# Convolution, output gate and new keys and values made beside the projection's products; level products from 64 rows per head

## The reference

```python
x = LN(x);  z = x @ w_in              # 3088 columns: gq gk gv gr glow sq sk sv cb cc ch
# A: gated linear attention, 4 heads, dk 64, dv 128, chunks of 64 tokens
lg  = log_sigmoid(glow @ w_gate_up + b_gate) / 16;  b = cumsum(lg) in a chunk
att = sum_k q[t,k] k[s,k] exp(b[t,k] - b[s,k]),  s <= t
o   = (q exp(b)) S + att v;   S = exp(b_last) S + (k exp(b_last - b))^T v
go  = rms_norm(o) * gla_norm_g * silu(gr)
# B: stick-breaking attention, 4 heads x 64, causal, over all keys up to t
so  = sum_s sigmoid(z[t,s]) prod_{s<r<t} (1 - sigmoid(z[t,r])) v[s],  z = q k / 8
# C: u = cc * ch;  co = cb * (w2 u[t] + w1 u[t-1] + w0 u[t-2])
x = LN(2^.25 x + concat(go, so, co) @ w_out)
x = LN(2^.25 x + relu(x @ w_up)^2 @ w_down)
```

## Time and profile before

| | us |
|---|---|
| median of 3 runs | 3113.41 (3110.74 to 3117.24) |
| profiled execution | 3112.73, its span 3110.9 |
| TensorE busy | 2734.4 (88% of the span) |
| TensorE weight loads | 2268.3 (73%) |
| VectorE busy | 1505.1 (48%) |
| ScalarE busy | 1069.5 (34%) |
| GpSimd busy | 329.9 (11%) |
| moved by DMA | 526.11 MB, mean 169 GB/s |

### The profile page before, as it was taken

One profiled execution on the slowest core, in us unless ns is written; L12 is line 12 of the kernel. 1 busy time (PEld: TensorE's weight loads), 2 busy tenths in 40 slices (PEclk: granted clock), 3 DMA queues, 4 the chain that ended last, 5 costly groups with the idle time before them and its releaser, 6 DMA issues. The chain is left out here.

```text
span 3110.9 us, 38667 instructions
## 1 busy us (share of the span) xinstructions
PE 2734.4 (88%) x13838; PEld 2268.3 (73%) x13838; DVE 1505.1 (48%) x2247; ACT 1069.5 (34%) x1783; POOL 329.9 (11%) x283
## 2 busy tenths in 40 slices
PE   5999999946662467999998999999999988999997
PEld 4787789835541356888877888877888766888885
DVE  5333342158883556665656544446644425522224
ACT  3323333223342424443443444443434321322221
POOL 1100010056600000000001100001100000000000
PEclk9999999966786588999999999999999989999998
DMA  5544454233315654575655766565766554544452
GB/s 185 169 160 153 160 180 126 85 121 88 89 45 187 191 191 140 169 249 179 216 193 191 229 218 209 191 206 183 234 190 227 170 171 144 190 157 158 154 168 98
DMA packets 362107, 526.11 MB, mean 169 GB/s; under 512 B 28832, under 2 KB 208208, under 8 KB 361920
## 3 DMA queue, kind: packets, MB, share of 16 engines
q1 hardware_dynamic: 337696, 480.23, 48.1%
q10 hardware_dynamic: 18832, 26.10, 2.3%
q0 software_dynamic: 5392, 17.31, 1.6%
HBM read 422.74 MB, written 100.80 MB: 168 GB/s over the span
## 5 line engine op out<-in xcount | busy, mean ns | idle before, releaser
L111 PE MATMUL p_ps_u<-p_xh,p_wh 128*128 128x512 f32 (+1 forms) x1280 | 453.1, 354 | 5.4 <-DVE p_xl L1626 5.4
L112 PE MATMUL p_ps_u<-p_xh,p_wl 128*128 128x512 f32 (+1 forms) x1280 | 451.5, 353 | 0.0
L113 PE MATMUL p_ps_u<-p_xl,p_wh 128*128 128x512 f32 (+1 forms) x1280 | 451.0, 352 | 0.0
L1575 DVE SCALAR_TENSOR_TENSOR p_res<-p_res,p_ps_d 128x512 f32<-128x512 f32 (+1 forms) x340 | 232.1, 685 | 451.4 <-PE p_ps_d L113 445.7
L111 PE MATMUL p_ps_d<-p_wh,p_hh 128*128 128x512 f32 (+1 forms) x1088 | 433.2, 398 | 16.9 <-DVE p_res L1575 14.8
L112 PE MATMUL p_ps_d<-p_wh,p_hl 128*128 128x512 f32 (+1 forms) x1088 | 428.6, 394 | 0.0
L113 PE MATMUL p_ps_d<-p_wl,p_hh 128*128 128x512 f32 (+1 forms) x1088 | 428.4, 394 | 0.0
L1484 ACT ACTIVATE p_wh<-p_wst 128x1024 fp32r<-128x1024 f32 x288 | 293.9, 1049 | 276.6 <-PE p_ps_d L113 225.0
L1633 DVE TENSOR_TENSOR p_r<-p_r 128x512 f32<-128x512 f32 (+1 forms) x160 | 95.8, 599 | 461.3 <-ACT p_hh L1514 461.3
L1507 ACT ACTIVATE p_r<-p_ps_u 128x512 f32<-128x512 f32 (+1 forms) x160 | 83.8, 524 | 579.5 <-PE p_ps_u L113 579.4
L111 PEld LDWEIGHTS p_ps_u<-p_xh,p_wh 128*128 128x128 f32 x1280 | 241.2, 188 | 35.5 <-DVE p_xl L1626 6.2
(11 more groups left out here) (155 smaller groups left out, 4473.0 us busy)
## 6 DMA issues: line engine op xcount, KB each, us to landing
p_wl<-wlo_scratch SPq DMA_DIRECT2D x216, 512.0 KB, 5.1
p_wst<-in_w_up SPq DMA_DIRECT2D x128, 512.0 KB, 6.0
p_wst<-in_w_down SPq DMA_DIRECT2D x128, 512.0 KB, 4.6
wlo_scratch<-p_wl SPq DMA_DIRECT2D x72, 512.0 KB, 3.6
p_wst<-in_w_in SPq DMA_DIRECT2D x128, 256.0 KB, 3.6
p_kk<-ks_scratch SPq DMA_DIRECT2D x84, 256.0 KB, 5.9
p_vv<-vs_scratch SPq DMA_DIRECT2D x84, 256.0 KB, 4.5
p_wst<-in_w_out SPq DMA_DIRECT2D x32, 512.0 KB, 6.0
```

Source lines behind the costliest of these rows:

```text
L111: pe.matmul(out, lhs_hi, rhs_hi, start=first, stop=False, skip_group_check=skip)
L112: pe.matmul(out, lhs_lo, rhs_hi, start=False, stop=False, skip_group_check=skip)
L113: return pe.matmul(out, lhs_hi, rhs_lo, start=False, stop=last, skip_group_check=skip)
L1575: dve.scalar_tensor_tensor(out=acc, in0=acc, scalar=scale, in1=ps_d[:c, d % DB, :], op0=ALU.mult, op1=ALU.add).then_inc(d_free, 1)
```

## The change

In `phase_in` the chunks come in another order (gv, gq with gk, gr with glow, keys with values, cc with ch, sq with cb). All steps are single: one slice of weights, one unit, one store. The weight slices of the next chunk are put three at a time before a unit, the store of a unit after the next unit. The first units need one tile each. The norm has two three-operand passes and GpSimd's power in place of ScalarE's root. ScalarE evacuates gr with a sigmoid and VectorE multiplies by gr and gla_norm_g / 8. cc, ch and cb stay in PSUM and one staging buffer, and VectorE makes the convolution and the gated product, which goes to `mixt_scratch`. Keys and values are stored as outputs, and their halves are made there too: values in place, keys by two transposes a tile (`kturn`), one unit later. There are six output slots.

`phase_gla` loads the gate ready made and has no convolution; `qb` and `qs` are laid out as the keys are, and level products and `inter` take 64 rows per head. In `phase_tail` one piece, the cache, is prepared.

```diff
-    chunks = [
-        ([(C_GQ, 512)], "F", Z_GQ),
-        ([(C_GR, 528)], "F", Z_GR),
-        ([(C_GV, 512)], "T", "gv"),
-        ([(C_SQ, 256), (C_CB, 256)], "F", Z_SQ),
-        ([(C_SK, 512)], "T", "kv"),
-        ([(C_CC, 512)], "F", Z_CC),
-    ]
...
+    chunks = [([(C_GV, 512)], "T"), ([(C_GQ, 512)], "F"), ([(C_GR, 528)], "F"), ([(C_SK, 512)], "T"), ([(C_CC, 512)], "F"),
+              ([(C_SQ, 256), (C_CB, 256)], "F")]
...
+        order = [("x_load", 0), ("consts",), ("x_load", 1), ("norm_a", 0), ("norm_b", 0), ("norm_a", 1), ("turn", 0)]
+        order += [("w", 0, k) for k in range(4)] + [("x_load", 2), ("norm_b", 1), ("x_load", 3)] + [("w", 0, k) for k in range(4, KT)]
...
+                if gc == 0:
+                    if x:
+                        order += [("norm_b", x + 1)] * (x + 1 < len(us)) + [("turn", x)]
+                    order += [("norm_a", x + 2)] * (x + 2 < len(us))
+                    if x == 1:
+                        order += [("x_load", j) for j in ahead]
...
+                order += more[3 * x:3 * x + 3]
+                order.append(("unit", i))
+                order += late.pop(0)
+                late.append([])
+                if units[i]["kind"] not in ("cc", "ch"):
+                    late[0].append(("store", i))
+                if units[i]["kind"] == "kv":
+                    late[0].append(("kturn", i))
+                    late[1].append(("kstore", i))
...
+                    dve.scalar_tensor_tensor(out=xn[:c, sl, :], in0=xs[:c, sl, :], scalar=mv[:c, sl, 0:1], in1=g_b[:c, :], op0=ALU.subtract, op1=ALU.mult).then_inc(scaled, 1)
+                    dve.wait_ge(rstd_done, j + 1)
+                    dve.wait_ge(scaled, j + 1)
+                    dve.scalar_tensor_tensor(out=xn[:c, sl, :], in0=xn[:c, sl, :], scalar=rstd[:c, sl:sl + 1], in1=b_b[:c, :], op0=ALU.mult, op1=ALU.add).then_inc(normed, 1)
...
+                    if kind in ("z", "silu"):
+                        act.activation(slot[:u["mw"], :u["n"]], ps[:u["mw"], :u["n"]], ACT.Sigmoid if kind == "silu" else ACT.Copy).then_inc(a_out, 1)
+                    else:
+                        act.activation(slot[:u["n"], :], ps[:u["n"], :], ACT.Copy).then_inc(a_out, 1)
+                    if kind == "kv":
+                        wait_slot(act, x + 1)
+                        vs = outb[:u["n"], (x + 1) % OUTS, :].bitcast(F32R).rearrange("p (h d) -> p h d", h=SBH)
+                        act.activation(vs[:, :, 0:64], ps[:u["n"], 256:512].rearrange("p (h d) -> p h d", h=SBH), ACT.Copy).then_inc(a_out, 1)
...
+                    ks = outb[:, x % OUTS, :].bitcast(F32R).rearrange("p (a e t) -> p a e t", a=2, e=2)
+                    for e in range(2):
+                        act.activation(ks[0:64, :, e, :n], ps_t[64 * e:64 * e + 64, q, 0:256].rearrange("p (a t) -> p a t", a=2)[:, :, :n],
...
+                    elif kind == "silu":
+                        slot, h = outb[:, slot_no[i] % OUTS, :u["n"]], u["m0"] // P
+                        dve.wait_ge(a_out, a_no[i])
+                        dve.wait_ge(gn_scaled, 1)
+                        dve.scalar_tensor_tensor(out=slot, in0=ps[:, :u["n"]], scalar=gn[:, h:h + 1], in1=slot, op0=ALU.mult, op1=ALU.mult).then_inc(d_out, 1)
...
+                            dve.tensor_tensor(cu[:, x, at_u + 2:at_u + 2 + n], ps[:, c:c + n], cin[:, c:c + n], ALU.mult).then_inc(d_out, 1)
...
+                            dve.tensor_scalar(y, cu[:, x, at_u + 2:at_u + 2 + n], cw[:, x, 2:3], None, ALU.mult).then_inc(conv_step, 1)
+                            for w in range(2):
+                                n_step += 1
+                                dve.wait_ge(conv_step, n_step)
+                                dve.scalar_tensor_tensor(out=y, in0=cu[:, x, at_u + w:at_u + w + n], scalar=cw[:, x, w:w + 1], in1=y,
+                                                         op0=ALU.mult, op1=ALU.add).then_inc(conv_step, 1)
...
+                            dve.tensor_tensor(outb[:, slot_no[i] % OUTS, c:c + cnt], ps[:, c:c + cnt], cy[:, x, o + c:o + c + cnt], ALU.mult).then_inc(d_out, 1)
...
+                    pool.tensor_tensor(rstd[:c, sl:sl + 1], veps[:c, sl:sl + 1], power[:c, :], ALU.pow).then_inc(rstd_done, 1)
...
+                        mm = pe.transpose(ps_t[:, q, p * P:p * P + n], outb[:n, slot_no[i] % OUTS, p * P:p * P + P], ident[:n, :n])
+                    mm.then_inc(k_turned, 1)
...
-                    act.activation(gg[:, q, :, :n], gr[:, :, :n], ACT.Exp, scale=-1.0).then_inc(r_exp, 1)
...
-                    for e in range(2):
-                        r = slice(64 * e, 64 * e + 64)
-                        dve.tensor_tensor(qs[r, q, :, e, :n], eb[r, q, :, :n], gq[r, q, :, :n], ALU.mult).then_inc(qs_done, 1)
+                    dve.wait_ge(consts_set, 3)
...
-                    for h in range(HEADS):
-                        last = dve.scalar_tensor_tensor(out=gg[:, q, h, :n], in0=gr[:, h, :n], scalar=gn[:, h:h + 1], in1=gg[:, q, h, :n],
-                                                        op0=ALU.mult, op1=ALU.mult)
...
-                    for e in range(2):
-                        r = slice(64 * e, 64 * e + 64)
-                        dve.tensor_tensor(qb[r, x % EX, :, e, :n // 2].rearrange("p a (b h) -> p a b h", h=hs), e2[r], q2[r], ALU.mult).then_inc(lev_mul, 1)
+                    dve.tensor_tensor(qb[:, x % EX, :, :n // 2].rearrange("p a (b h) -> p a b h", h=hs), e2, q2, ALU.mult).then_inc(lev_mul, 1)
...
-                            for n, t in enumerate(ts):
-                                cols = slice(t * P, t * P + w)
-                                if li < NL:
-
-                                    wo = w // 2
-                                    mm = pe.matmul(ps_l[:w, e, n * w:n * w + w], ex[:, x % EX, e, cols], qb[:, x % EX, e, :, t * wo:t * wo + wo],
-                                                   start=n == 0, stop=n == len(ts) - 1, skip_group_check=True)
-                                    continue
-
-                                r = slice(64 * e, 64 * e + 64)
-                                for pr in range(2):
-                                    at_ = (pr * len(ts) + n) * w
-                                    mm = pe.matmul(ps_l[:w, e, at_:at_ + w], gk[r, g % 2, pr, cols], gq[r, g % 2, pr, cols],
-                                                   start=n + pr == 0, stop=n + pr == len(ts), skip_group_check=True)
+                            for pr in range(2):
+                                for n, t in enumerate(ts):
+                                    cols = slice(t * P, t * P + w)
+                                    if li < NL:
+                                        wo = w // 2
+                                        at_ = (pr * len(ts) + n) * wo
+                                        mm = pe.matmul(ps_l[:w, e, at_:at_ + wo], ex[r, x % EX, pr, cols], qb[r, x % EX, pr, t * wo:t * wo + wo],
+                                                       start=n + pr == 0, stop=n + pr == len(ts), skip_group_check=True)
+                                    else:
+                                        at_ = (pr * len(ts) + n) * w
+                                        mm = pe.matmul(ps_l[:w, e, at_:at_ + w], gk[r, g % 2, pr, cols], gq[r, g % 2, pr, cols],
+                                                       start=n + pr == 0, stop=n + pr == len(ts), skip_group_check=True)
...
+                        for e in range(2):
+                            r, at_ = slice(64 * e, 64 * e + 64), m * pr + x * CHUNK
+                            mm = pe.matmul(ps_o[:, e, at_:at_ + CHUNK], st[r, before(c), pr, :], qs[r, q, pr, cols],
+                                           start=False, stop=x == len(cs) - 1, skip_group_check=True)
...
-                pool.tensor_tensor(u[:, 2:2 + n], cc[:, sl_, :n], ch[:, :n], ALU.mult).then_inc(c_u, 1)
...
-        order += [("p_load", 0), ("q_load", 0), ("p_load", 1), ("pk", 0, 0), ("pk", 0, 1), ("pv", 0), ("p_store", 0), ("p_load", 2), ("q_prep", 0), ("k_load", 0)]
-        steps = []
-        for c in range(1, 6):
-            steps += [[("pk", c, 0)], [("pk", c, 1)], [("pv", c)], [("p_store", c)] + ([("p_load", c + 2)] if c < 4 else [])]
+        order += [("q_load", 0), ("k_load", 0), ("p_load",), ("q_prep", 0)]
+        steps = [[("pk", 0)], [("pk", 1)], [("pv",)], [("p_store",)]]
         for n, x in enumerate(steps):
             add_attention(group_end[0] * (n + 1) // (len(steps) + 1))
             order += x
-            if n == 3:
+            if n == 0:
...
-                    sp.wait_ge(prep_out, PREP_STORES * (un["chunk"] + 1))
+                    if un["chunk"] == 4:
+                        sp.wait_ge(prep_out, PREP_STORES)
...
```

More of the change, by code:

```diff
@@ L177, in phase_in @@
             n += len(gtiles[-1])
-        units = []
+        NT = n
+        units, by_chunk = [], []
         for g, (t0, cnt) in enumerate(GROUPS):
-            for c, (pieces, kind, where) in enumerate(chunks):
```

(63 more changed lines are left out.)

671 lines of the change are left out of this document (342 added, 329 removed).

## The result

The changed kernel is slower: 3178.82 us median of 4 runs (3170.6 to 3181.63) against 3112.07 us (3110.27 to 3117.24) for the kernel before on the same chip, a ratio of 1.0206 with a 95% interval of 1.0189 to 1.0223. The forecast was 2988 us, with a range of 2955 to 3035. Its profiled execution has a span of 3179.8 us, 68.9 more than before.

What follows compares the result with a forecast made beforehand. TensorE bounds the projection and the stretch after 1110.54 us, VectorE linear attention, a chain of waits the last phase's opening. Terms -1 - 69 - 55 = -125 from 3112.7 gave 2988 us, range 2955 to 3035.

Steps and rivals of the forecast that it cites:

- Opening of the projection: Projection's start: first product at some 15 us instead of 42.29, gain 6 us; bounds a gain of 15, a loss of 3.
- Work beside the products: Projection: key transposes add 5 us on TensorE; added vector work, ScalarE work and stores stay hidden, priced at nothing.
- the slower rival: Projection: each of 119 products waits 1.5 us for its own evacuation, 178 us in all, giving 3166; chance 0.04.
- VectorE's relief of 8.7 us a group: Linear attention: fewer query, decay and gate passes cut a full group from 55.66 to 47 us.
- The idle 4 us: Linear attention: VectorE's remaining 4 us of idleness per full group, from the gate's ScalarE chain, was to stay.
- Convolution off GpSimd: Linear attention: without GpSimd's contention groups 1 and 2 match group 3; -69 us including VectorE's relief, bounds -50 and -78.
- part 3: Linear attention: VectorE's saving of 8.7 us per full group from merged query and decay passes and dropped gate passes.
- Level products: Linear attention: 16 records a level become 32 of 64 rows by 64 columns, at the same total cost.
- I take the lower end: Linear attention: each 64-row record costs half, so a level's sum is unchanged; upper end 7.5 and 4.1 us a level.
- The second rival: Linear attention: 64-row products cost the full record, +19 in group 0, +5 in each other, giving 3022; chance 0.10.
- Opening of the last phase: Before 1110.54 us: five of six key-value preparations go, 154.84 becomes 99.5, gain 55; bounds -35 and -66.
- The better bounds of the parts it names: Range's low end, 2955: better bounds for VectorE's relief, the convolution move and the last phase's opening.

Runs made afterwards that it cites:

- e1: Changed kernel with level products and products with the state put back to 128 rows: 3086.33 us, ratio 0.9908.
- e6: e1 with the output gate's load issued late, behind the last tile's store of group g-2: 3051.66 us, ratio 0.9804.
- e8: Changed kernel with 128-row products, the output gate's load late and the tile's transposes ahead of the keys': 3038.78 us, ratio 0.977.
- e7: Changed kernel with the next token tile's transposes moved ahead of the new keys' transposes: 3161.74 us, ratio 1.0159.
- e9: e4 with the output gate's load late and the tile's transposes ahead of the keys': 3084.86 us, ratio 0.9911.
- e11: Kernel before the change, with the convolution's arithmetic on GpSimd left out, its loads and stores kept: 3088.1 us, ratio 0.9926.
- e13: e8 with the next group's gate product and logarithm moved earlier, behind the last level product but one: 3023.24 us, ratio 0.9713.
- e5: Changed kernel with the output gate's load issued late, behind the last tile's store of group g-2: 3145.67 us, ratio 1.0102.
- e2: 128-row kernel with each 128-column level product made as two of 64 columns, 32 records a level: 3121.38 us, ratio 1.002.
- e4: Changed kernel with 64-row level products reordered so the two heads' halves alternate: 3125.66 us, ratio 1.0038.

## Why the prediction was wrong, point by point

The changed kernel is 190.8 us over the forecast. By the experiments 92.5 of that go with the 64-row products (e1), 34.7 with the gate's load (e6 against e1), 12.9 with the order of the two turns (e8 against e6), and 50.8 are left in e8.

1. Opening of the projection: the mechanism was right. First product at 15.40, and about 7 us ahead of the kernel before at 100 us, counted in products (259 against 230 at 0.231 us each).

2. Work beside the products: "I price all this at nothing" held for the vector work, and the slower rival never came: no wait for an evacuation beyond the keys'. What failed is the price of the keys' transposes, 5 us. They cost 34 records as said, and beside that a stall of up to 3.2 us in three places, because they take a bank that the tile's turn needs next (13 us with the clock's fall, e7). The stage came out at +12.5 instead of -1; in e8, with the turn moved, it ends at 635.8 us, 2 before the kernel before. I had looked at banks for products, not at the two for transposes.

3. VectorE's relief of 8.7 us a group: VectorE's busy time in group 3 fell by 6.6 us (51.67 to 45.12), in e9 by 7.6 (44.03). The count had been a little high: by its own rows a level gains 2 x 683 - 688 = 678 ns, 4.1 us for six and not 4.5. That it "comes off the group" is where the step fails: e8, at 128 rows with the gate's four passes gone, is 3.8 us under e11 in the whole stage. The idle 4 us did not stay 4: with 49 us of work a group takes 55 to 62. e13 shows that a good part was the gate's chain at the group's head, which I had kept at its size in a group where nothing else was late.

4. Convolution off GpSimd: the contention is real and its total was met, in part by luck. e11 gives 28.5 us in the stage where the prediction's share without part 3 was 8.5 + (133.50 - 2 x 55.66) = 30.7. But groups 1 and 2 did not come down to what group 3 takes: they gave 11.7 us and not 22.2, and group 0 gave 17.0 and not 8.5. The two errors nearly cancel. In group 0 the granted clock rose as well, from 0.55 to 0.73. What it lacked is the move of the gate's load: it listed what SyncE loses, not that a load with a later wait stands ahead of values. 33 and 35 us (e5, e6).

5. Level products: this is the step that turned the sign. "I take the lower end" put 32 records at the price of 16; they took 5.4 us, between the ends of 3.75 and 7.5. The row used for it, two products 0.10 us apart, was of operands split in two parts, one record a product; the levels' products are of plain f32, two records each, and e2 has them at 0.215 us with 64 columns where 128 columns cost 0.236, so the columns alone do not set their price. The Trainium skill's rule on row groups ("TensorE: Matmul & The Clock Gate", The mechanism), which I set aside on that row, points the right way for them, as e4 shows; the 7.5 us that I had read out of it did not come. Worse than the price was the clock, which the sum took from the kernel before. The levels' records doubled, a group has 404 of TensorE where it had 276, and at a clock of 0.50 to 0.54 they keep it busy for 72 to 77 us of each group, so VectorE waits for them. The second rival named the mechanism and priced it 34 us (+19 in group 0, +5 in three others), with the upper level assumed from group 1 on; e1 makes it 92.5. By order 53 of that, by the products with the state some 6; the 33 left are the clock and the wait for both banks together (e4).

6. Opening of the last phase: -40 instead of -55. The mechanism was right, ScalarE no longer waits for stores of prepared keys. VectorE's timeline has the first and the last two heads' outputs at

```profile
1099.82 0.42 DVE L1778 TENSOR_TENSOR p_ob<-p_ps_o,p_otmp 64x256 f32<-64x256 f32 x1
...
1145.08 0.41 DVE L1778 TENSOR_TENSOR p_ob<-p_ps_o,p_otmp 64x256 f32<-64x256 f32 x1
1158.58 0.41 DVE L1778 TENSOR_TENSOR p_ob<-p_ps_o,p_otmp 64x256 f32<-64x256 f32 x1
```

The first output comes 37.7 us after the phase begins. TensorE's first product is at 13.1 us (12 in the sum). Then the four weight slices, which the sum has at 10, come in the middle of the first head: ScalarE is with them for 11.7 us, and TensorE stands for 12.0. ScalarE's timeline, and TensorE's next product:

```profile
1086.20 1.99 ACT L1577 ACTIVATE p_wh<-p_wst 128x1024 fp32r<-128x1024 f32 x2
1094.26 1.06 ACT L1577 ACTIVATE p_wh<-p_wst 128x1024 fp32r<-128x1024 f32 x1 [6.06 <-DMA p_wst<-in_w_out]
1096.81 1.06 ACT L1577 ACTIVATE p_wh<-p_wst 128x1024 fp32r<-128x1024 f32 x1 [1.50 <-DMA p_wst<-in_w_out]
...
1098.48 0.26 PE L1878 MATMUL p_ps_z<-p_causalb,p_identb 128*128 128x128 bf16 x1 [12.04 <-ACT p_sg L1633]
```

That leaves 13.0 us for the first head, where the sum had its pace of 7. The seven steps after it take 58.8 us against 53 for seven heads and the preparation. So of the miss of 15.2 us, 6.0 lie in the first head, 5.8 in the seven steps, and the rest in the first operands, the weights and the end. The pace came from pairs of heads (the trace has four of them, not five); here three of the seven steps are longer, 10.3, 10.7 and 13.5. The last stands behind the preparation's five stores in SyncE's queue. No run tests this part.

7. The rest: 2003.01 against 2000.36, 0 as said.

The range was not added up as it says. The better bounds of the parts it names give 2988 - 9 - 11 = 2968; only with the projection's 14 does it come to 2954. And 3035 is the second rival with the projection's poorer bound, not two rivals.

Without points 5 and the gate's load, and with the turn moved, the change does most of what was forecast: e8 at 3039 is 51 us over 2988, some 37 of it in the groups (262.7 us against 226) and 15 in the last opening. The remaining groups of 55 us after e13, with 49 of VectorE, are not taken apart further. What exactly raises the granted clock stays open: in these runs it is low with 64-row products and higher with full-height ones, but e2's group 0 stays low with full height.

## What to carry to other kernels

Before a product is cut to half the rows, ask whether TensorE may become the bound: price it with the weight load shown, and at the lower clock level, and let neighbouring products use different halves of the rows. When a load moves to another buffer, write down its new wait and everything behind it in that queue. Work taken from the busiest engine gives back less than its size once a chain at the head of each group lasts longer than the slack, so read that chain first.

## What was not expected of the hardware

- Plain f32 products of 128 rows cost 0.215 us a record with 64 moving columns and 0.236 with 128 at the lower clock level (0.115 and 0.126 at the upper).
- The same 64-row, 64-column record costs 0.169 us behind one of its own rows and 0.115 behind one of the other half.
- TensorE worked 31.85 us without a gap on 64-row products and stayed at a granted clock of 0.50; eight full-height products ahead of each level brought the groups to 0.61 to 0.81.
- Three stalls of 3.2 us at most in the projection, 9.3 in all, put its end off by 13 us on average; the clock was 0.89 and 0.94 in the 20 us around the first.
